# The modulation vectors of a four-layer model: from POOL's products to a multiply-and-sum on VectorE

## What is computed

```python
c_act = jax.nn.silu(c)                      # (1, 1024)
mod = (c_act @ w_ada + b_ada)[:, None, :]   # w_ada: (1024, 6144), one for each second layer
sh1, sc1, g1, sh2, sc2, g2 = jnp.split(mod, 6, axis=-1)
h = rms_norm_2(x, norm1_g) * (1 + sc1) + sh1
```

## Time and profile before

| | |
|---|---|
| median of three runs | 3586.69 us (3580.44 to 3594.11) |
| the profiled execution | 3591.43 us; its span 3590.0 us, from the first to the last instruction |
| engines busy | PE 3048.6 us (85%), DVE 2451.5 (68%), ACT 1484.2 (41%), POOL 975.7 (27%) |
| granted TensorE clock, mean | 0.917 |
| two first layers | 23 to 735 us and 735 to 1450 us |
| second mixer and expert stage, first pass | 1452 to 2516 us |
| second mixer and expert stage, second pass | 2524 to the end |
| POOL's products L690 | 48, 214.8 us busy |
| POOL's sums L692 | 144, 266.5 us busy |
| DVE's taps L774 | 480, 312.0 us busy, mean 721 ns |
| DVE's rests L721 | 156, 392.1 us busy, mean 2529 ns; idle before them 194.1 us, for ACT's heads |

### The profile page before, as it was taken

The page is one execution under the profiler, slowest core; times in us unless marked ns, Lnnn a source line. Parts: engine busy times, 40 slices in busy tenths (PEclk is TensorE's granted clock), DMA queues, the critical chain, the costliest instruction groups (busy, mean ns, idle before and its releaser), DMA issues. The chain is left out here.

```text
span 3590.0 us, 48390 instructions
## 1 busy us (share of the span) xinstructions
PE 3048.6 (85%) x18164; PEld 2711.3 (76%) x18164; DVE 2451.5 (68%) x3911; ACT 1484.2 (41%) x2252; POOL 975.7 (27%) x537
## 2 busy tenths in 40 slices
PE   6764799867658998777997999999677987999998
PEld 5664677666546776667987998888667987998887
DVE  5998766569987665446959655665446959555665
ACT  2221453222214432234457444554234457444554
POOL 3355520443555205005960000000006950000000
PEclk9887999988878999778999999999778999999999
DMA  5443444454434444514551566665505641566665
GB/s 206 157 145 136 176 170 145 168 214 145 150 142 170 169 142 167 185 46 153 184 153 48 157 189 184 205 194 169 188 31 166 184 140 48 175 189 185 205 194 162
DMA packets 128232, 568.89 MB, mean 158 GB/s; under 512 B 14155, under 2 KB 24172, under 8 KB 96364
## 3 DMA queue, kind: packets, MB, share of 16 engines
q1 hardware_dynamic: 117916, 505.43, 43.1%
q0 software_dynamic: 9216, 56.63, 4.4%
q10 hardware_dynamic: 864, 3.67, 0.3%
HBM read 551.52 MB, written 15.20 MB: 158 GB/s over the span
## 5 line engine op out<-in xcount | busy, mean ns | idle before, releaser
L1811 PE MATMUL e_ps<-k_hhi,e_hi 128*128 128x256 f32 x2304 | 651.8, 283 | 30.0 <-POOL e_lo L1796 30.0
L1811 PE MATMUL e_ps<-k_hlo,e_hi 128*128 128x256 f32 x2304 | 646.1, 280 | 0.0
L1811 PE MATMUL e_ps<-k_hhi,e_lo 128*128 128x256 f32 x2304 | 644.6, 280 | 0.0
L2069 DVE TENSOR_TENSOR e_lo<-e_raw,e_hi 128x1024 fp32r<-128x1024 f32 x394 | 482.8, 1225 | 203.5 <-ACT e_hi L1893 202.8
L1893 ACT ACTIVATE e_hi<-e_raw 128x1024 fp32r<-128x1024 f32 x544 | 570.9, 1049 | 27.9 <-DMA e_raw<-down 27.0
L721 DVE TENSOR_TENSOR f_wlo<-f_raw,f_whi 128x2048 fp32r<-128x2048 f32 x156 | 392.1, 2529 | 194.1 <-ACT f_whi L539 194.1
L539 ACT ACTIVATE f_whi<-f_raw 128x2048 fp32r<-128x2048 f32 x156 | 296.4, 1912 | 506.8 <-DMA f_raw<-ws 395.7
L1811 PEld LDWEIGHTS e_ps<-k_hhi,e_hi 128*128 128x128 f32 x2304 | 436.6, 189 | 31.7 <-POOL e_lo L1796 31.3
L1811 PEld LDWEIGHTS e_ps<-k_hlo,e_hi 128*128 128x128 f32 x2304 | 436.5, 189 | 0.0
L1811 PEld LDWEIGHTS e_ps<-k_hhi,e_lo 128*128 128x128 f32 x2304 | 436.0, 189 | 0.0
L1796 POOL TENSOR_TENSOR e_lo<-e_raw,e_hi 128x1024 fp32r<-128x1024 f32 x150 | 384.3, 2577 | 89.4 <-ACT e_hi L1893 88.4
(11 more groups left out here) (337 smaller groups left out, 5607.4 us busy)
## 6 DMA issues: line engine op xcount, KB each, us to landing
f_raw<-ws SPq DMA_DIRECT2D x156, 1024.0 KB, 5.0
e_raw<-down SPq DMA_DIRECT2D x288, 512.0 KB, 3.7
e_raw<-up SPq DMA_DIRECT2D x256, 512.0 KB, 3.6
f_x<-ada POOLq DMA_DIRECT2D x48, 1024.0 KB, 5.3
s_raw<-ws SPq DMA_DIRECT2D x24, 1024.0 KB, 5.0
mod_parts<-f_x POOLq DMA_DIRECT2D x48, 128.0 KB, 2.0
s_parts<-mod_parts SPq DMA_DIRECT2D x8, 768.0 KB, 9.5
f_x<-out SPq DMA_DIRECT2D x4, 1024.0 KB, 5.1
```

Source lines behind the costliest of these rows:

```text
L1811: last = nc.tensor.matmul(psD(n), w, h, start=kt == 0 and i == 0, stop=kt == KT - 1 and i == 2)
L2069: V.tensor_tensor(lo[:, i % RING, :], raw[:, i % RING, :], hi[:, i % RING, :].bitcast(F32), ALU.subtract).then_inc(S["lo_dve"], 1)
```

## The change

The matrix is transposed on the host, so that row block a of `w_ada` transposed, 128 output columns on the partitions by 1024 inputs, is one tile of 512 KB. 48 such tiles (`MODS`) make a layer's `mod`. `c_act` is kept as a row, repeated on all partitions, in DRAM (`c_row`), and is loaded into the second half of `f_x` once a layer. For each tile SP loads it into the first half of `f_x`, and DVE multiplies it by the row and sums along the row in one instruction (`scalar_tensor_tensor` with `accum_out`), which gives one column of `MOD` (128 x 48). The tile's place in both orders is tied to the weight units: tile a goes with unit u = 28 + a. On SP it is loaded just ahead of unit u, behind a wait for the modulation of the tile before (`ada_done`), as there is one buffer. On DVE its modulation stands just behind the rest of unit u. SP's loop over the units is written out. At the layer's end SP stores `MOD` (`mod_cols`) before it reloads x.

POOL keeps only its small inverse roots and memsets. The second mixer loads `mod_cols` (24 KB) instead of the parts; PE's 48 matmuls go; DVE adds `b_ada` in place. `prepare` works on c as 128 x 1024 and stores `c_row`.

```diff
+MODS = 48
+ADA_FROM = 28
+def ada_tile(u):
+    a = u - ADA_FROM
+    return a if 0 <= a < MODS else None
...
-    ada = Xr[:, :, :].rearrange("p t n -> p (t n)")
+    ada, c_row = Xr[:, 0, :], Xr[:, 1, :]
...
-                with sp.Fori(1, U1 // NRAW) as i:
-                    for k in range(NRAW):
-                        sp.wait_ge(S["lo_ready"], i * NRAW + (k + 1 - NRAW))
-                        load(i * NRAW + k, k)
-
-                sp.wait_ge(env["out_ada"], l * (16 * ADA_U) + 16 * ADA_U)
+                for u in range(NRAW, U1):
+                    if u == ADA_FROM:
+                        sp.wait_ge(S["x_norm"], NT)
+                        sp.dma_start(c_row, inp["c_row"]).then_inc(S["in_crow"], 16)
+                    a = ada_tile(u)
+                    if a is not None:
+                        if a:
+                            sp.wait_ge(S["ada_done"], a)
+                        sp.dma_start(ada, inp["ada"][bass.ds(l * MODS + a, 1), :, :].rearrange("o p n -> p (o n)")).then_inc(S["in_ada"], 16)
+                    sp.wait_ge(S["lo_ready"], u + 1 - NRAW)
+                    load(u, u % NRAW)
+
+                sp.wait_ge(S["ada_done"], MODS)
+                sp.dma_start(inp["mod_cols"][bass.ds(l, 1), :, :].rearrange("o p n -> p (o n)"), MOD).then_inc(S["out_mod"], 16)
                 sp.dma_start(Xr[:, :, :], x_dram).then_inc(S["in_x"], 16)
+                sp.wait_ge(S["out_mod"], 16)
...
-                pool.wait_ge(S["x_norm"], NT)
-                def modulation(u):
...
-                for u in range(5):
-                    modulation(u)
...
-                for u in range(5, ADA_U - 4):
-                    modulation(u)
...
-                for u in range(ADA_U - 4, ADA_U):
-                    modulation(u)
...
+                def modulation(u):
+                    a = ada_tile(u)
+                    if a is not None:
+                        if a == 0:
+                            dve.wait_ge(S["in_crow"], 16)
+                        dve.wait_ge(S["in_ada"], 16 * (a + 1))
+                        V.scalar_tensor_tensor(ada, ada, 1.0, c_row, ALU.mult, ALU.mult, accum_out=MOD[:, a:a + 1]).then_inc(S["ada_done"], 1)
...
                         V.tensor_tensor(w_lo[:, u % NW, :], raw[:, u % NRAW, :], w_hi[:, u % NW, :].bitcast(F32),
                                         ALU.subtract).then_inc(S["lo_ready"], 1)
                         converted[0] += 1
+                        modulation(u)
...
+                act.wait_ge(S["c_ready"], 1)
+                act.dma_start(inp["c_row"], c_act[:, :]).then_inc(S["c_out"], 16)
                 act.wait_ge(S["bias_out"], 16)
+                act.wait_ge(S["c_out"], 16)
...
-                quarter = ADA_U // 4
-                for i in range(4):
-                    sp.dma_start(parts[:, i * quarter:(i + 1) * quarter, :],
-                                 inp["mod_parts"][bass.ds(l * ADA_U + i * quarter, quarter), :, :].rearrange("u p n -> p u n")).then_inc(S[f"in_parts{i}"], 16)
+                sp.dma_start(mod[:, :], inp["mod_cols"][bass.ds(l, 1), :, :].rearrange("o p n -> p (o n)")).then_inc(S["in_mod"], 16)
...
-                for c in range(48):
-                    if c % 12 == 0:
-                        pe.wait_ge(S[f"in_parts{c // 12}"], 16)
-                    last = nc.tensor.matmul(psA[:, 3, c:c + 1], parts[:, c // 2, (c % 2) * P:(c % 2 + 1) * P], ones[:, 0:1], start=True, stop=True)
-                last.then_inc(S["mod_mm"], 1)
...
-                dve.wait_ge(S["mod_mm"], 1)
-                own.link(V.scalar_tensor_tensor(mod[:, :], psA[:, 3, 0:48], 256.0, par["b_ada"], ALU.mult, ALU.add))
+                dve.wait_ge(S["in_mod"], 16)
+                own.link(V.tensor_tensor(mod[:, :], mod[:, :], par["b_ada"], ALU.add))
```

More of the change, by code:

```diff
@@ L292, in first_layer @@
             s_ready s_masked s_negmax s_exp s_sink pt_ready pt_read o_ready m_add
-            decay_exp dec_arg dec_ready ro_ready r_var r_rstd r_og m_done x_done out_x""".split()
+            decay_exp dec_arg dec_ready ro_ready r_var r_rstd r_og m_done x_done out_x in_crow in_ada ada_done out_mod""".split()
         S = {n: cx.enter_context(nc.semaphore("f_" + n)) for n in names}
@@ L677, in _ @@
                 rstd(RS, SS, NT, 1.0 / D, S["x_rstd"])
-                pool.wait_ge(S["x_norm"], NT)
-                def modulation(u):
-                    place = inp["ada"][bass.ds(l * ADA_U + u, 1), :, :].rearrange("o p n -> p (o n)")
-                    if u:
-                        pool.wait_ge(env["out_ada"], l * (16 * ADA_U) + u * 16)
-                    pool.dma_start(ada, place).then_inc(env["in_ada"], 16)
-                    pool.wait_ge(env["in_ada"], l * (16 * ADA_U) + (u * 16 + 16))
-                    a3 = ada.rearrange("p (k n) -> p k n", k=KT)
-                    by_c = env["c_act"][:, :].rearrange("p (k n) -> p k n", n=1).to_broadcast([P, KT, 256])
-                    own.link(nc.gpsimd.tensor_tensor(a3, a3, by_c, ALU.mult))
-                    for half in (1024, 512, 256):
-                        own.link(nc.gpsimd.tensor_tensor(ada[:, 0:half], ada[:, 0:half], ada[:, half:2 * half], ALU.add))
-                    parts = inp["mod_parts"][bass.ds(l * ADA_U + u, 1), :, :].rearrange("o p n -> p (o n)")
-                    pool.dma_start(parts, ada[:, 0:256]).then_inc(env["out_ada"], 16)
-                for u in range(5):
-                    modulation(u)
                 for i in range(6):
@@ L1047 @@
 P2OFF, P2N = offsets(P2)
-ADA_U = 24
 def prepare(nc, env, inp):
-    x_dram, c_act = env["xd"], env["c_act"]
+    x_dram = env["xd"]
     pb = arena(nc, env["base"])
-    c_in = pb("p_c", [P, KT])
-    c_tanh = pb("p_ctanh", [P, KT])
+    c_in = pb("p_c", [P, D])
+    c_tanh = pb("p_ctanh", [P, D])
+    c_act = pb("p_cact", [P, D])
     rel = pb("p_rel", [P, H2])
@@ L1135, in second_mixer @@
     g1 = pb("s_g1", [P, D])
-    late_at = pb.at[0]
-    parts = pb("s_parts", [P, ADA_U, 256], offset=late_at)
     qn = pb("s_qn", [P, NT, CH])
@@ L2223, in second_arrays @@
             ws2[l * U2 + u] = unit_array(weights[w][l], r0, c0, layout)
-        for u in range(ADA_U):
-            ada[l * ADA_U + u] = unit_array(w_ada_2[l], 0, 256 * u, "B")
+        ada[l * MODS:(l + 1) * MODS] = w_ada_2[l].T.reshape(MODS, P, D)
         rows = dict(b_ada=columns(b_ada_2[l]), norm1_g=columns(norm1_g_2[l]), norm2_g=columns(norm2_g_2[l]), gain=columns(out_norm_g_2[l]),
@@ L2240, in second_arrays @@
         pick[bucket[u] if valid[u] else 32, u] = 1.0
-    return dict(c=np.ascontiguousarray(columns(c_2[0])),
+    return dict(c=np.tile(c_2[0], (P, 1)),
                 rel=rel_bias_2, pick=pick, ada=ada, par2=par, ws2=ws2,
```

17 lines of the change are left out of this document (8 added, 9 removed).

## The result

| | before | after |
|---|---|---|
| median | 3583.8 us (3580.4 to 3594.1) | 3844.9 us (3840.8 to 3846.1) |
| ratio, with its 95% interval | | 1.072 (1.070 to 1.075) |
| the profiled execution, its span | 3591.4, 3590.0 us | 3840.8, 3839.2 us |
| DVE, ACT, POOL busy | 2451.5, 1484.2, 975.7 us | 2339.3, 1486.3, 438.5 us |
| granted TensorE clock, mean | 0.917 | 0.894 |

DVE and POOL have less to do, and the kernel takes 261 us more. The forecast was 3842. (The median of before is here of four runs; the prediction had three of them, 3586.69 us.)

The account below looks back on a forecast made before the run. DVE was taken to bound the first layers' convolution, PE the attention's pairs. First layers +284, second mixers -30, preparation +1: +255 on the profiled 3591.4 gives 3846, expected median 3842 us, range 3795 to 3940.

Parts of the forecast that it names:

- The link: First layers, units 29 to 75: each load waits for the previous unit's load, rounding, subtraction and modulation; 11.8 us a unit.
- The landing: Within each link: tile and unit land 6.15 us after the tile's issue, ends 5.5 and 7.4.
- the first rival: DVE's modulation runs at half rate because it keeps a sum: 1.05 us more each, +100, 3942 us; chance 0.08.
- POOL's products: First layer, 63 to 278 us: without them DVE's taps fall from 689 to 476 ns; -53 us a layer.
- The attention's pairs: First layer, 409.3 to 514.05 us: seven pairs at two links each, 4 us allowed for PE's clock; 172 us, +68.
- The retention and the branches: First layer, 514.05 to 700.4 us: 23 links plus DVE work and ends, 297.2 us instead of 186.3, +111.
- the cover: The 8.27 us of each link that can hide DVE's other work between two units.
- The second mixer: Dropping the parts' four transfers and 48 one-column products brings L1492 earlier: -15 us a layer, -30 for two.
- Preparation: Before the layers: c becomes 512 KB and its activated row is stored; +1.3 us for 0.5 MB more to land.
- The end of the layer: First layer's end: two small SP transfers land beside PE's last units, and nothing changes; 0 us.
- The third rival: Loads keep enough lead to hide the chain, so only POOL's removal and the mixers count: 3420 us; chance 0.03.
- break-even link: Link length at which the change neither gains nor loses: 9.1 us, 2.7 below the forecast link.

Follow-up runs that it names:

- The third experiment: The kernel before without POOL's product and its three sums, tile loads and stores kept: 3394.1 us, ratio 0.947.

## Why the prediction was right, step by step

Stretches of the first layer, read in the profiled executions (a unit's end is that of its rest, after the change that of its modulation):

| from, to | before | after | difference | forecast |
|---|---|---|---|---|
| block start to rest 28 | 270.0 | 209.9 | -60.1 | -53 |
| rest 28 to the last tap | 51.6 | 46.0 | -5.6 | -7 |
| last tap to the end of unit 37 | 64.5 | 89.9 | +25.4 | +23 |
| to the end of unit 51 | 104.8 | 169.1 | +64.3 | +68 |
| to the last addition of the branches | 186.3 | 299.1 | +112.8 | +111 |
| from there to the next layer | 34.8 | 38.6 | +3.8 | 0 |
| the layer | 711.9 | 852.6 | +140.7 | +142 |

The second first layer went from 716.9 to 847.1 (+130, where +142 was forecast: its stretch before rest 28 fell by 59 instead of 53, and its attention's pairs grew by 61.6 instead of 68), the two second layers by -14.1 and -10.2, and what lies before the first block by +2.7. Together +249 between the two spans, where +255 was forecast.

- **The link.** Forecast 0.1 + 6.15 + 1.92 + 0.1 + 2.2 + 1.33 = 11.8; measured 0.17 + 6.20 + 1.91 + 0.03 + 2.21 + 1.23 = 11.75 in the link shown above, median of all 11.77. The landing, the one term that no row had in this form, came out at 6.18 (median) against 6.15: it could be put together from the rows of a lone 512 KB transfer and of the second of two 1 MB loads. The ends I had given it, 5.5 and 7.4, weren't needed for the median, but eleven landings lay above 6.3 us from the load's issue, which lifts the mean from the tile's issue to 6.35. A unit's load starts 0.70 us (median) behind the modulation before it, 1.05 at most.
- **The modulation's rate.** This was the first rival, and two lines of the trace decide it (ns min/median/max, first and last start):

```profile
L718 DVE SCALAR_TENSOR_TENSOR f_x<-f_x x96: 1217/1219/1224, 238.0 to 1686.2; 128x1024 f32<-128x1024 f32 x96
L718 DVE DVE_READ_ACCUMULATOR f_x<-f_x x96: 81/83/89, 239.2 to 1687.4; 128x1 f32 x96
```

  1219 ns, not 2300: the rate of the earlier trace rows holds with a sum too. The read-out is 83 ns, not ACT's 186, and covered in most part; the term was 0.1 us too high. The Trainium skill (Vector Engine (DVE) Microarchitecture Reference, Points that are easy to get wrong) says that this operation with two non-bf16 SBUF sources halves its throughput. Read as twice the time of these rows, as the prediction read it, this doesn't hold here: a subtraction of the same width without a sum, L2064 of the changed kernel, takes 1225 ns in the mean. Whether the sentence is meant against a faster rate of bf16 sources no run here shows, as all data is fp32; the measurement decides.
- **POOL's products.** The taps' mean came to 486 ns (from 689), as forecast to 10 ns. The stretch fell by 60, not 53: my sum ended at 278 us, while the stretch that I compared with ended at rest 28, 293.2, and POOL's share between the two was left out. The third experiment finds the same 59.6 us with nothing else changed. It also shows that the whole cost, some 96 us a layer, is larger than what the changed kernel shows, since in the later stretches the chain covers it.
- **The attention's pairs.** Twice 11.75 for each of seven, 1 us more for each of the two pairs with an eviction on DVE, some 3 for slow landings: 169.1. My own terms give 171.6 us and so +67, not +68. The 4 us in them for PE's clock were not needed. The granted clock did fall, to 0.82 in this stretch, and the pairs without an eviction or a slow landing took the length of two links (23.3 to 23.8 us).
- **The retention and the branches.** The sum of 23 links and 7.6 us of work over the cover gave 297.2; measured it is 299.1. One landing of 6.9 us and one of 6.7 (5.65 is the median) would make up the difference.
- **The second mixer.** From its start to L1487 (L1492 before): 17.7 us after 32.3 in the first pass and 18.6 after 33.1 in the second, with the bias transfer landing last: -14.6 a layer for -15.
- **Preparation.** +2.7 instead of +1.3. ACT stores the bias rows at 18.52 us instead of 17.23. PE's bias products, which they wait for, start at 4.49 us instead of 3.20, released by a small transfer (`p_pick`) that now lands beside c's 512 KB. The second store behind it on the same queue, for which the block's end waits too, lands another 1.3 us later (24.89 against 23.61). I had counted 0.5 MB once, and it is moved twice.
- **The end of the layer.** 0 was wrong by 3 us for the first layer, for a reason that the trace of before couldn't show: SP's written-out program.
- **The third rival's time.** For the case that loads kept their lead I had worked out 3420 us; the version with the later modulation took 3405. Its break-even link was 9.1 us, the experiments put it near 8.9 by estimate.

So the steps held: the chain, its length and its count are what the runs show. That 3842 met 3844.9 to 3 us is luck in part. The errors went both ways: the taps' stretch gave 6 to 7 us a layer more than forecast, the second layer's pairs took 6 us less and the modulation was 0.1 us a link shorter, while the slow landings, the layer's end and the preparation cost more. The medians are 261 us apart and the two profiles 249, with 255 forecast, so the forecast can't be said to be good to better than some 6 us.

## What to carry to other kernels

A wait put into a queue delays all that stands behind it, not only the transfer it was made for. Here one buffer for a side task turned a stream with two buffers into a chain of one, at some 100 us per us of link, and moving two lines in SP's order took back 377 of the 440 us it cost. Where a step also shortened the cover that hides other work, it gave less (106 us for a link 1.2 us shorter). Before such a wait is placed, write down the loop that it closes (issue, landing, each engine's step, the instruction that releases it), count its passes, and compare its length with the pace at which the kernel runs now; if the loop can be closed one unit later, close it there, and put the side transfer behind the main one. The engine that a change relieves (POOL, and with it DVE: 193 us) and the queue that it loads have to be priced apart, since here the gain was real and was covered by a loss of more than twice its size.

## What the runs showed of the hardware that I hadn't expected

- POOL's element-wise arithmetic on SBUF made DVE's instructions longer, by 217 us of busy time, and the kernel by 193 us in 3587. POOL's issue of the same transfers cost little that shows: a tap took 482 ns with it and 689 with the arithmetic too, and 486 in the changed kernel without either.
- The sum of a row kept by a multiply on DVE costs 83 ns for its read-out, most of it covered; the 1024-wide instruction with fp32 inputs from SBUF took 1219 ns, and the 64-wide one 0.22 us.
- A 64 KB transfer ahead of a 1 MB one delayed the latter's landing by its 0.53 us of issue and by nothing else that shows: the unit landed 4.83 us behind its own issue, and 4.88 where it stood first. With 512 KB ahead it was 0.8 us more.
- A written-out order of 78 units on SP cost 3 us at the outer loop's jump back (8.2 and 8.7 us against 5.4 with inner loops).
- In the changed kernel 26 of 94 loads met a packet on an instruction queue, and those landed later by 0.6 us in the mean (6.27 against 5.64 us), one by nearly 3. Whether the packet is the cause was not tested.
